# Recurrent mixer: three ScalarE roundings moved later, input-gate products and three low parts moved to GpSimd

## The chip, the cores and the metric

The kernel runs on one core of a Trainium2 chip as one program. The metric is the device time of one execution in microseconds, the median over several runs. The engines are TensorE (PE in the profile), VectorE (DVE), ScalarE (ACT), GpSimd (POOL) and the queue that issues most transfers (SyncE, SP).

## The reference, cut to what matters

A sequence of 256 positions with 1024 channels passes through a first block of two layers (an attention mixer, then a recurrent mixer, each followed by a feed-forward part) and a second block of two layers. All is float32. The change touches the recurrent mixer of the first block alone:

```
gate_branch, xr = jnp.split(x @ w_in, 2, axis=-1)
xr = causal_dwconv(xr, conv_w, conv_b)                 # 4 taps
r = sigmoid(blocks(xr) @ w_a + b_a)                    # recurrence gate
i = sigmoid(blocks(xr) @ w_x + b_x)                    # input gate
log_a = (-LRU_C * r) * softplus(-lam);  a = exp(log_a)
u = sqrt(-expm1(2.0 * log_a)) * (i * xr)
h = scan(h = a * h + u) over the positions
y = (h * gelu(gate_branch)) @ w_out
```

## The kernel before

Channels lie on the 128 partitions and the 256 positions on the free axis, so that a tensor of 1024 channels is eight tiles of 128x256. Each matrix product is done as three float32r products: weights and activations are split into a high part (rounded) and a low part (the remainder), and high x high, high x low and low x high are added in PSUM.

Weights come as 313 chunks of 128x2048, one MB each, through three raw buffers and a ring of four split buffers. SP issues the transfer of chunk n when the low part of chunk n-3 is written (it then owns the raw buffer). ScalarE rounds a chunk to its high part (`round_chunk`, line 224), VectorE subtracts (`rest_chunk`, line 233), and TensorE multiplies. `refill_hi(act, c)` rounds the chunk four after c, since it reuses the slot of c; `refill_lo(dve, c)` makes the low part of the chunk three after c. Every engine has one queue in program order, written out by hand, so a rounding that stands early in ScalarE's list holds all that stands behind it.

In the recurrent mixer TensorE does, in this order: four chunks `od_xr` (recurrent branch; chunks 53 to 56), `od_gate0` (57), two chunks `od_ax` (58, 59) with the gate matrices, in eight steps j of 12 matmuls each (6 for `r`, 6 for `i` of tile j), three chunks `od_gate` (60 to 62), and `od_out` (63 to 66). Step j > 3 reuses the PSUM bank of step j-4 and so waits for the sigmoid `i{j-4}`; it also waits for the low part of the branch, `lo{j//2}`. The first two chunks of `od_out` go through `alternating` (lines 291 and 298): all products with the high part of y, tile by tile, each waiting for `yhi`, then those with the low part, each waiting for `ylo`. They start when the low parts of both chunks 63 and 64 and `yhi0` are there. The next stage, `up1`, follows on TensorE without a pause.

`odd_act` is ScalarE's list (from line 1161): last taps, high parts of the branch (`xr_high`), sigmoids (line 1186), the group of Exp, Tanh and Square for each pair of tiles (lines 1231 to 1235), Sqrt (1238), Gelu (1191) and the high parts of y (1196), with the roundings between them. `odd_dve` is VectorE's (from line 1512): taps (1531), low parts of the branch (1537), `decay(j)` with the log of the decay `la` (1566) and the product of input gate and branch `ux` (1568), `v` (1578), `scan(h)` with `u` (1586) and two scans (1591), the gated output `y` (1597) and its low part (1602), with `take_scaled` (318, which empties a PSUM bank) and the low parts of the chunks between them. GpSimd does nothing in this stage. In the feed-forward stages it multiplies and makes low parts (lines 849, 855), and later it scales residuals (371).

Of the kernel before, what the change touches and what calls it, by code (L numbers as in the profile page):

```python
# [164 lines left out]
def program(nc, x_in, stream, par1_in, par2_in, ev_const, mask_const, mats, inv_in, out):  # L165
    with ExitStack() as ctx:
# [59 lines left out]
        def refill_hi(act, c):  # L226

            round_chunk(act, c.number + RING)
# [700 lines left out]
        def conv_names(g):  # L929
            return [f"{t}{d}_{g}" for d in (1, 2, 3) for t in "ab"]  # L930

        ax_names = [[f"r{j}", f"i{j}"] for j in range(8)]
        od_act = Steps(sem("od_act"), ["a_0", "b_0", "a_1", "b_1", "hi0", "hi1", "a_2", "b_2", "hi2", "a_3", "b_3"] +
                       sum(ax_names[:2], []) + ["hi3"] + sum(ax_names[2:], []) +
                       sum(([f"a{h}", f"tanh{h}", f"a2{h}"] for h in G4), []) + [f"sqrt{h}" for h in G4] +
                       ["gelu0", "gelu1", "yhi0", "yhi1", "gelu2", "yhi2", "gelu3", "yhi3"])
        od_dve = Steps(sem("od_dve"), conv_names(0) + conv_names(1) + ["lo0", "lo1"] + conv_names(2) + ["lo2"] +
                       conv_names(3) + ["lo3"] + sum(([f"la{j}", f"ux{j}"] for j in range(8)), []) +
                       [f"v{h}" for h in G4] +
                       ["u0", "scan00", "scan01", "u1", "scan10", "scan11", "y0", "y1", "ylo0",  # L940
                        "u2", "scan20", "scan21", "ylo1", "y2", "u3", "scan30", "scan31", "ylo2", "y3", "ylo3"])
        ax_done = sem("ax_step_done")

        def windows():
# [215 lines left out]
        def odd_act(act):  # L1160
# [53 lines left out]
            xr_high(2)  # L1214
            last_tap(3)
            act.activation(small[:, 6:7], eps, ACT.Sigmoid)
            act.wait_ge(chunk_done, gate0.number + 1)
            refill_hi(act, gate0)
            sigmoids(0)
            sigmoids(1)  # L1220
            xr_high(3)
            sigmoids(2)
            sigmoids(3)
            refill_hi(act, Chunk("od_ax", 0))
            for j in range(4, 8):
                sigmoids(j)
            refill_hi(act, Chunk("od_ax", 1))
            act.wait_ge(*A.after("i7"))
            for h in G4:
                act.wait_ge(*od_dve.after(f"ux{2 * h + 1}"))  # L1230
                act.activation(S(TMP + 2 * h, 2), S(RR + 2 * h, 2), ACT.Exp).then_inc(*A.did(f"a{h}"))
                act.activation(S(RR + 2 * h, 2), S(RR + 2 * h, 2), ACT.Tanh, scale=-1.0)\
                   .then_inc(*A.did(f"tanh{h}"))
                act.wait_ge(*A.after(f"a{h}"))
                act.activation(S(XC + 2 * h, 2), S(TMP + 2 * h, 2), ACT.Square).then_inc(*A.did(f"a2{h}"))
            for h in G4:
                act.wait_ge(*od_dve.after(f"v{h}"))
                act.activation(S(RR + 2 * h, 2), S(RR + 2 * h, 2), ACT.Sqrt).then_inc(*A.did(f"sqrt{h}"))
# [275 lines left out]
        def odd_dve(dve):  # L1514
            V = od_dve
            xr = [Chunk("od_xr", g) for g in G4]
            gate0 = Chunk("od_gate0", 0)
            gate = [Chunk("od_gate", g) for g in range(3)]

            def branch(g):  # L1520
                take_scaled(dve, xr[g], S(TMP + 2 * xr[g].slot, 2))

            def conv(g):
                dve.wait_ge(*od_act.after(f"b_{g}"))
                for d in (1, 2, 3):
                    for t, nm in enumerate("ab"):
                        k = 2 * g + t
                        if d > 1:
                            dve.wait_ge(*V.after(f"{nm}{d - 1}_{g}"))
                        w = PAR1["odw"] + 4 * k + 3 - d  # L1530
                        dve.scalar_tensor_tensor(out=scr[:, XC + k, d:T], in0=scr[:, TMP + 2 * xr[g].slot + t, 0:T - d],
                                                 scalar=par1[:, w:w + 1], in1=scr[:, XC + k, d:T],
                                                 op0=ALU.mult, op1=ALU.add).then_inc(*V.did(f"{nm}{d}_{g}"))

            def xr_low(g):
                dve.wait_ge(*od_act.after(f"hi{g}"))
                dve.tensor_tensor(hs[:, 8 + 2 * g:10 + 2 * g, 1, :], S(XC + 2 * g, 2),
                                  hs[:, 8 + 2 * g:10 + 2 * g, 0, :].bitcast(F32), ALU.subtract)\
                   .then_inc(*V.did(f"lo{g}"))

            refill_lo(dve, xr[0])
            inverse_dve(dve, N["mixnorm1"], 0)
            refill_lo(dve, xr[1])
            dve.wait_ge(*N["mixnorm1"]["stat"].after("copied"))
            branch(0)
            branch(1)
            conv(0)
            conv(1)
            xr_low(0)
            branch(2)  # L1550
            refill_lo(dve, xr[2])
            xr_low(1)
            conv(2)
            branch(3)
            refill_lo(dve, xr[3])
            xr_low(2)
            conv(3)
            take_scaled(dve, gate0, S(GB, 2))
            xr_low(3)
            refill_lo(dve, gate0)  # L1560
            cc = small[:, 24:32]

            def decay(j):

                dve.wait_ge(*od_act.after(f"i{j}"))
                dve.tensor_scalar(S1(RR + j), S1(RR + j), cc[:, j:j + 1], -8.0, ALU.mult, ALU.mult)\
                   .then_inc(*V.did(f"la{j}"))
                dve.tensor_tensor(S1(II + j), S1(II + j), S1(XC + j), ALU.mult).then_inc(*V.did(f"ux{j}"))
            for j in range(4):
                decay(j)  # L1570
            refill_lo(dve, Chunk("od_ax", 0))
            for j in range(4, 8):
                decay(j)
            refill_lo(dve, Chunk("od_ax", 1))
            for h in G4:

                dve.wait_ge(*od_act.after(f"a2{h}"))
                dve.scalar_tensor_tensor(out=S(RR + 2 * h, 2), in0=S(XC + 2 * h, 2), scalar=1.0,
                                         in1=S(RR + 2 * h, 2), op0=ALU.add, op1=ALU.mult).then_inc(*V.did(f"v{h}"))
                if h == 0:  # L1580
                    take_scaled(dve, gate[0], S(GB + 2, 2))
                    refill_lo(dve, gate[0])

            def scan(h):
                dve.wait_ge(*od_act.after(f"sqrt{h}"))
                dve.tensor_tensor(S(II + 2 * h, 2), S(II + 2 * h, 2), S(RR + 2 * h, 2), ALU.mult)\
                   .then_inc(*V.did(f"u{h}"))
                dve.wait_ge(*V.after(f"u{h}"))
                for k in range(2):
                    t = 2 * h + k  # L1590
                    dve.tensor_tensor_scan(S1(XC + t), S1(TMP + t), S1(II + t), 0.0, ALU.mult, ALU.add)\
                       .then_inc(*V.did(f"scan{h}{k}"))

            def gated(h):
                dve.wait_ge(*od_act.after(f"gelu{h}"))
                dve.wait_ge(*V.after(f"scan{h}1"))
                dve.tensor_tensor(S(GB + 2 * h, 2), S(GB + 2 * h, 2), S(XC + 2 * h, 2), ALU.mult)\
                   .then_inc(*V.did(f"y{h}"))

            def lo(h):  # L1600
                dve.wait_ge(*od_act.after(f"yhi{h}"))
                dve.tensor_tensor(hs[:, 2 * h:2 * h + 2, 1, :], S(GB + 2 * h, 2),
                                  hs[:, 2 * h:2 * h + 2, 0, :].bitcast(F32), ALU.subtract)\
                   .then_inc(*V.did(f"ylo{h}"))
            scan(0)
            take_scaled(dve, gate[1], S(GB + 4, 2))
            scan(1)
            refill_lo(dve, gate[1])
            gated(0)
            gated(1)  # L1610
            lo(0)
            scan(2)
            lo(1)
            gated(2)
            scan(3)
            take_scaled(dve, gate[2], S(GB + 6, 2))
            lo(2)
            gated(3)
            lo(3)
            refill_lo(dve, gate[2])  # L1620

        def pool_means(pool, l):

# [161 lines left out]
        def _(pool):  # L1785
# [14 lines left out]
            pool.wait_ge(*ev_dve.after("glo"))  # L1800
            pool.dma_start(S(INV, 4), inv_in).then_inc(inv_landed, 16)
            up_pool(pool, "up0", FF1, U["up0"], 0)
            up_pool(pool, "up1", FF1, U["up1"], 0)
            pool.wait_ge(inv_landed, 16)
            residual_pool(pool, PN["final"], 0, gains("final"))
# [9 lines left out]
        def _(pe):  # L1815
# [26 lines left out]
            for q in range(2):  # L1842
                c = Chunk("od_ax", q)
                pe.wait_ge(lo_ready, c.number + 1)
                for s in range(4):
# [6 lines left out]
                             signal=(chunk_done if s == 3 else ax_done, 1))  # L1852
            whole_pe(pe, "od_gate", 3, 0)
            out_pe(pe, "od_out", 1, hs, 8, lambda k: od_act.after(f"yhi{k // 2}"),
                   lambda k: od_dve.after(f"ylo{k // 2}"), 0, tr=O["od_out"])
            pre_pe(pe, [("up1", FF1)], N["ffnnorm1"], summed(O["od_out"]), 0)
            out_pe(pe, "down1", 3, hs, FF1, None, hs_ready(U["up1"], 0), 0, tr=O["down1"])

# [305 lines left out]
```

## Time and profile before

| what | value |
|---|---|
| median of 3 runs | 1913.71 us (1913.6 to 1913.81) |
| the profiled execution, own time | 1914.2 us |
| its span | 1912.4 us |
| mean granted TensorE clock | 0.987 of full |
| PE, DVE, ACT, POOL busy | 97%, 75%, 51%, 11% of the span |

The profiled execution took 1.8 us more than its span, and 0.5 us more than the median of the timed runs. Times in the rows below count from the start of the span. The recurrent mixer lies at about 396 to 476 us of it. Busy time of an engine is summed over its instructions. Successive instructions on one engine overlap a little, so the step from one start to the next is shorter than the duration shown.

### The profile page before, as it was taken

The numbers are of one execution on the slowest core, as the hardware profiler recorded it, in microseconds if no ns is written. First come the engines' busy times: TensorE is split into PE (matmuls) and PEld (weight loads), VectorE is DVE, ScalarE is ACT, GpSimd is POOL, SyncE is SP. The second block draws the span as 40 slices with busy tenths as digits, with TensorE's granted clock in tenths as the row PEclk, the third lists the DMA queues.
The fourth block names the chain that finished last, engine by engine and source line by source line (L and its number), as shares of the span: only waits on it lengthen the run. The fifth ranks groups of instructions, "written<-read, shape, count | busy, mean of one in ns | idle before, by whom it ended". The sixth has DMA issues, their size and how long they took to land.

```text
span 1912.4 us, 31584 instructions
## 1 busy us (share of the span) xinstructions
PE 1845.5 (97%) x13170; PEld 1730.8 (91%) x13170; DVE 1427.6 (75%) x1728; ACT 974.7 (51%) x1179; POOL 216.3 (11%) x160
## 2 busy tenths in 40 slices
PE   7978999999999999999999999999999999999997
PEld 7958999998999898889999988898889999998887
DVE  5796998578799568757875687758775886578774
ACT  5453765467666455544453455545554445345552
POOL 0020332000232012002300020002000220002000
PEclk9989999999999999999999999999999999999999
DMA  7413555534455545554454445554555445445551
GB/s 284 152 45 119 178 183 194 199 133 163 169 197 188 187 166 187 185 212 160 171 198 177 176 155 186 209 200 141 190 194 217 142 177 197 155 154 199 182 215 67
DMA packets 46788, 334.65 MB, mean 175 GB/s; under 512 B 5184, under 2 KB 5568, under 8 KB 6464
## 3 DMA queue, kind: packets, MB, share of 16 engines
q1 hardware_dynamic: 46512, 332.20, 48.2%
q8 instruction: 104, 1.70, 0.3%
q0 software_dynamic: 144, 0.52, 0.1%
q14 instruction: 28, 0.23, 0.0%
HBM read 331.65 MB, written 1.05 MB: 174 GB/s over the span
## 4 chain that ended last, share of the span: by engine, by line
PE 84%; DVE 11%; ACT 2%; issue 1%; DMA 1%; SPq 0%; DVEq 0%; ACTq 0%
PE psum L267 25%; PE psum L270 13%; PE psum L251 12%; PE psum L252 12%; PE psum L253 12%; PE psum L291 5%; DVE w_lo L233 3%; PE psum L298 3%; DMA w_raw<-stream_in 1%; DVE x_resid L476 1%; PE psum L585 1%; PE psum L584 1%; PE psum L582 1%; DVE x_split L408 1%; ACT w_hi L224 1%
## 5 line engine op out<-in xcount | busy, mean ns | idle before, releaser
L224 ACT ACTIVATE w_hi<-w_raw 128x2048 fp32r<-128x2048 f32 x313 | 598.2, 1912 | 459.5 <-PE psum L253 218.0
L233 DVE TENSOR_TENSOR w_lo<-w_raw,w_hi 128x2048 fp32r<-128x2048 f32 x313 | 726.6, 2324 | 44.1 <-ACT w_hi L224 44.1
L251 PE MATMUL psum<-x_split,w_hi 128*128 128x256 f32 x1768 | 504.4, 285 | 11.8 <-DVE x_split L408 10.5
L252 PE MATMUL psum<-x_split,w_hi 128*128 128x256 f32 x1768 | 500.9, 283 | 0.0
L253 PE MATMUL psum<-x_split,w_lo 128*128 128x256 f32 x1768 | 500.8, 283 | 0.0
L267 PE MATMUL psum<-x_split,w_hi 128*128 128x512 f32 x1216 | 430.2, 399 | 3.5 <-DVE scratch L318 3.5
L251 PEld LDWEIGHTS psum<-x_split,w_hi 128*128 128x128 f32 x1768 | 339.9, 192 | 13.9 <-issue 12.8
L270 PE MATMUL psum<-x_split,w_lo 128*128 128x256 f32 x1216 | 341.5, 281 | 0.0
L252 PEld LDWEIGHTS psum<-x_split,w_hi 128*128 128x128 f32 x1768 | 339.9, 192 | 0.1
L253 PEld LDWEIGHTS psum<-x_split,w_lo 128*128 128x128 f32 x1768 | 339.9, 192 | 0.0
L267 PE MATMUL psum<-h_split,w_hi 128*128 128x512 f32 x816 | 288.6, 399 | 0.0
L267 PEld LDWEIGHTS psum<-x_split,w_hi 128*128 128x128 f32 x1216 | 228.5, 188 | 61.1 <-DVE scratch L318 4.3
L270 PEld LDWEIGHTS psum<-x_split,w_lo 128*128 128x128 f32 x1216 | 229.7, 189 | 0.0
L270 PE MATMUL psum<-h_split,w_lo 128*128 128x256 f32 x816 | 229.2, 281 | 0.0
L267 PEld LDWEIGHTS psum<-h_split,w_hi 128*128 128x128 f32 x816 | 153.3, 188 | 38.2
L371 POOL TENSOR_TENSOR x_resid<-x_resid,squares 128x512 f32<-128x512 f32 x24 | 63.0, 2655 | 873.1 <-DVE squares L360 873.0
L270 PEld LDWEIGHTS psum<-h_split,w_lo 128*128 128x128 f32 x816 | 154.1, 189 | 0.0
L318 DVE TENSOR_TENSOR scratch<-psum,inv_rms 128x512 f32<-128x512 f32 (+1 forms) x129 | 86.8, 682 | 76.0 <-PE psum L253 75.8
L251 PE MATMUL psum<-h_split,w_hi 128*128 128x256 f32 x480 | 138.7, 289 | 3.9 <-issue 2.0
L748 ACT ACTIVATE scratch<-psum 128x512 f32<-128x512 f32 x76 | 45.4, 598 | 187.1 <-PE psum L270 187.1
L252 PE MATMUL psum<-h_split,w_hi 128*128 128x256 f32 x480 | 136.9, 285 | 0.0
L253 PE MATMUL psum<-h_split,w_lo 128*128 128x256 f32 x480 | 136.8, 285 | 0.0
(233 smaller groups left out, 2434.6 us busy)
## 6 DMA issues: line engine op xcount, KB each, us to landing
w_raw<-stream_in SPq DMA_DIRECT2D x313, 1024.0 KB, 4.8
x_resid<-x_in SPq DMA_DIRECT2D x1, 1024.0 KB, 7.0
y_out<-x_resid SPq DMA_DIRECT2D x4, 256.0 KB, 2.5
scratch<-mask_in SPq DMA_DIRECT2D x1, 768.0 KB, 11.0
scratch<-ev_in SPq DMA_DIRECT2D x1, 512.0 KB, 9.6
scratch<-inv_in POOLq DMA_DIRECT2D x1, 512.0 KB, 3.9
params<-par_in SPq DMA_DIRECT2D x1, 247.0 KB, 7.1
matrices<-mat_in SPq DMA_DIRECT2D x1, 192.0 KB, 8.9
```

Of the source, the lines that this page charges most:

```text
L224: act.activation(w_hi[:, n % RING, :], raw[:, n % RAWS, :], ACT.Copy).then_inc(hi_ready, 1)
L233: dve.tensor_tensor(w_lo[:, n % RING, :], raw[:, n % RAWS, :], w_hi[:, n % RING, :].bitcast(F32), ALU.subtract).then_inc(lo_ready, 1)
L251: pe.matmul(dst, w_hi[:, c.slot, b:b + P], src[:, k0 + k, 0, :], start=opens, stop=False)
L252: pe.matmul(dst, w_hi[:, c.slot, b:b + P], src[:, k0 + k, 1, :], start=False, stop=False)
L253: done = pe.matmul(dst, w_lo[:, c.slot, b:b + P], src[:, k0 + k, 0, :], start=False, stop=last and k == nk - 1 and m == len(tiles_) - 1)
L267: pe.matmul(ps[:, bank_, :], w_hi[:, c.slot, b:b + P], src[:, k0 + k, :, :].rearrange("p a t -> p (a t)"), start=first and k == 0, stop=False)
L270: done = pe.matmul(tile(bank_, 0), w_lo[:, c.slot, b:b + P], src[:, k0 + k, 0, :], start=False, stop=last and k == nk - 1)
L291: pe.matmul(tile(c.bank, m), w[:, c.slot, b:b + P], src[:, k0 + k, 0, :], start=k == 0 and m == 0 and w is w_hi, stop=False)
L298: done = pe.matmul(tile(c.bank, m), w_hi[:, c.slot, b:b + P], src[:, k0 + k, 1, :], start=False, stop=k == nk - 1 and m == 1)
L318: dve.tensor_tensor(dst, bank(c.bank, tiles), rinv[:, :].unsqueeze(1).to_broadcast([P, tiles, T]), ALU.mult).then_inc(pair_taken, 1)
L371: pool.tensor_tensor(x[:, 2 * g:2 * g + 2, :], x[:, 2 * g:2 * g + 2, :], UNRMS.unsqueeze(1).to_broadcast([P, 2, T]), ALU.mult).then_inc(*t ...
L748: act.activation(S(ACC + 2 * c.slot, 2), ps[:, c.bank:c.bank + 2, T:2 * T], ACT.Copy)\
```

## The change

On ScalarE the roundings of chunks 61, 62 and 63 (`refill_hi` of `gate0`, `od_ax` 0 and 1) stand later: 61 behind all four of the first sigmoid pairs and `xr_high(3)`, 62 behind the Exp group of pair 1, and 63 behind that of pair 2. The Exp groups wait for `la` in place of `ux`, and the Square, which overwrites the branch, waits for `ux`.

The product `ux` leaves VectorE for GpSimd, one instruction of 128x256 for each of eight tiles, each waiting for its sigmoid `i{j}`. `la` now waits for `r{j}` alone. VectorE's low parts of chunks 60 to 63 move within its list: 60 behind the first four `la`, 61 behind the other four, 62 behind `v1` and the emptying of the first gate bank, 63 behind `v2`. Each scan also waits for GpSimd's product.

Of the four low parts of y, GpSimd makes the first three (128x512 each), VectorE the last. `gated(0)` stands ahead of the low part of chunk 64 instead of behind it, and the emptying of the last gate bank ahead of scan 3.

```diff
@@ odd_act
             act.activation(small[:, 6:7], eps, ACT.Sigmoid)
+            for j in range(4):
+                sigmoids(j)
+            xr_high(3)
             act.wait_ge(chunk_done, gate0.number + 1)
             refill_hi(act, gate0)
-            sigmoids(0)
-            sigmoids(1)
-            xr_high(3)
-            sigmoids(2)
-            sigmoids(3)
-            refill_hi(act, Chunk("od_ax", 0))
             for j in range(4, 8):
                 sigmoids(j)
-            refill_hi(act, Chunk("od_ax", 1))
-            act.wait_ge(*A.after("i7"))
             for h in G4:
-                act.wait_ge(*od_dve.after(f"ux{2 * h + 1}"))
+                act.wait_ge(*od_dve.after(f"la{2 * h + 1}"))
                 ...
                 act.wait_ge(*A.after(f"a{h}"))
+                act.wait_ge(*od_pool.after(f"ux{2 * h + 1}"))
                 act.activation(S(XC + 2 * h, 2), S(TMP + 2 * h, 2), ACT.Square).then_inc(*A.did(f"a2{h}"))
+                if h == 1:
+                    refill_hi(act, Chunk("od_ax", 0))
+                if h == 2:
+                    refill_hi(act, Chunk("od_ax", 1))
@@ odd_dve
             xr_low(3)
-            refill_lo(dve, gate0)
 ...
-                dve.wait_ge(*od_act.after(f"i{j}"))
+                dve.wait_ge(*od_act.after(f"r{j}"))
                 dve.tensor_scalar(S1(RR + j), ..., ALU.mult, ALU.mult).then_inc(*V.did(f"la{j}"))
-                dve.tensor_tensor(S1(II + j), S1(II + j), S1(XC + j), ALU.mult).then_inc(*V.did(f"ux{j}"))
             for j in range(4):
                 decay(j)
-            refill_lo(dve, Chunk("od_ax", 0))
+            refill_lo(dve, gate0)
             for j in range(4, 8):
                 decay(j)
-            refill_lo(dve, Chunk("od_ax", 1))
+            refill_lo(dve, Chunk("od_ax", 0))
             for h in G4:
                 ...                                    # v{h}
-                if h == 0:
+                if h == 1:
                     take_scaled(dve, gate[0], S(GB + 2, 2))
+                    refill_lo(dve, Chunk("od_ax", 1))
+                if h == 2:
                     refill_lo(dve, gate[0])
             def scan(h):
                 dve.wait_ge(*od_act.after(f"sqrt{h}"))
+                dve.wait_ge(*od_pool.after(f"ux{2 * h + 1}"))
 ...
             scan(1)
+            gated(0)
             refill_lo(dve, gate[1])
-            gated(0)
             gated(1)
-            lo(0)
             scan(2)
-            lo(1)
             gated(2)
+            take_scaled(dve, gate[2], S(GB + 6, 2))
             scan(3)
-            take_scaled(dve, gate[2], S(GB + 6, 2))
-            lo(2)
             gated(3)
-            lo(3)
+            ...                                        # ylo3, as lo(3) was
+        def odd_pool(pool):
+            for j in range(8):
+                pool.wait_ge(*od_act.after(f"i{j}"))
+                pool.tensor_tensor(S1(II + j), S1(II + j), S1(XC + j), ALU.mult).then_inc(*od_pool.did(f"ux{j}"))
+            for h in range(3):
+                pool.wait_ge(*od_act.after(f"yhi{h}"))
+                pool.tensor_tensor(hs[:, 2 * h:2 * h + 2, 1, :], S(GB + 2 * h, 2),
+                                   hs[:, 2 * h:2 * h + 2, 0, :].bitcast(F32), ALU.subtract)\
+                    .then_inc(*od_pool.did(f"ylo{h}"))
@@ gpsimd
             up_pool(pool, "up0", FF1, U["up0"], 0)
+            odd_pool(pool)
             up_pool(pool, "up1", FF1, U["up1"], 0)
```

## Rows read from the trace of the kernel before

**Rows 1.** The page, parts 1 and 4: busy time, chain of waits by engine.
```profile
PE 1845.5 (97%) x13170; PEld 1730.8 (91%) x13170; DVE 1427.6 (75%) x1728; ACT 974.7 (51%) x1179; POOL 216.3 (11%) x160
...
PE 84%; DVE 11%; ACT 2%; issue 1%; DMA 1%; SPq 0%; DVEq 0%; ACTq 0%
```

**Rows 2.** Timeline, TensorE: start us, us, instruction, [idle before <-releaser].
```profile
421.85 0.36 PE L251 MATMUL psum<-h_split,w_hi 128*128 128x256 f32 x1 [2.02 <-issue]
...
429.14 0.28 PE L251 MATMUL psum<-x_split,w_hi 128*128 128x256 f32 x1
...
450.55 0.46 PE L291 MATMUL psum<-h_split,w_hi 128*128 128x256 f32 x1 [3.97 <-ACT h_split L1196]
...
458.83 0.38 PE L291 MATMUL psum<-h_split,w_hi 128*128 128x256 f32 x1 [0.81 <-ACT h_split L1196]
```

**Rows 3.** Windows of 1 us: busy of PE, PEld, DVE, ACT, POOL, clock, DMA share, GB/s.
```profile
425.00:426.00 1.00, 1.00 (x7) 1.00 (x6) 1.00 (x2) 1.00 (x1) 0.00 (x0) 0.50 0.06 16
...
451.00:452.00 1.00, 1.00 (x7) 1.00 (x6) 0.96 (x3) 1.00 (x1) 0.00 (x0) 0.50 0.77 319
```

**Rows 4.** Timeline, ScalarE, same columns.
```profile
419.13 1.89 ACT L224 ACTIVATE w_hi<-w_raw 128x2048 fp32r<-128x2048 f32 x1
420.93 1.55 ACT L1186 ACTIVATE scratch<-psum,params 128x256 f32<-128x256 f32 x4
422.36 0.64 ACT L1176 ACTIVATE h_split<-scratch 128x512 fp32r<-128x512 f32 x1
...
432.84 1.28 ACT L1231 ACT_TABLE_LOAD   x1
...
441.81 2.19 ACT L1238 ACTIVATE scratch<-scratch 128x512 f32<-128x512 f32 x4
...
458.15 0.63 ACT L1196 ACTIVATE h_split<-scratch 128x512 fp32r<-128x512 f32 x1 [0.76 <-DVE scratch L1597]
```

**Rows 5.** Timeline, VectorE, same columns.
```profile
419.30 2.44 DVE L1531 SCALAR_TENSOR_TENSOR scratch<-scratch,params 128x255 f32<-128x255 f32 x6
...
423.64 2.29 DVE L233 TENSOR_TENSOR w_lo<-w_raw,w_hi 128x2048 fp32r<-128x2048 f32 x1
425.84 0.35 DVE L1566 TENSOR_SCALAR scratch<-scratch,small 128x256 f32<-128x256 f32 x1
426.11 0.42 DVE L1568 TENSOR_TENSOR scratch<-scratch 128x256 f32<-128x256 f32 x1
426.44 0.34 DVE L1566 TENSOR_SCALAR scratch<-scratch,small 128x256 f32<-128x256 f32 x1
...
439.25 1.97 DVE L1578 SCALAR_TENSOR_TENSOR scratch<-scratch 128x512 f32<-128x512 f32 x3
442.47 0.69 DVE L1586 TENSOR_TENSOR scratch<-scratch 128x512 f32<-128x512 f32 x1 [1.25 <-ACT scratch L1238]
...
450.44 0.69 DVE L1602 TENSOR_TENSOR h_split<-scratch,h_split 128x512 fp32r<-128x512 f32 x1
451.05 0.69 DVE L1586 TENSOR_TENSOR scratch<-scratch 128x512 f32<-128x512 f32 x1
```

**Rows 6.** Timeline, GpSimd, same columns.
```profile
502.08 2.61 POOL L849 TENSOR_TENSOR scratch<-scratch 128x256 f32<-128x256 f32 x1 [175.61 <-ACT scratch L726]
...
620.94 0.74 POOL L855 TENSOR_TENSOR h_split<-scratch,h_split 128x256 fp32r<-128x256 f32 x1 [0.53 <-ACT h_split L732]
621.64 2.79 POOL L849 TENSOR_TENSOR scratch<-scratch 128x256 f32<-128x256 f32 x1
...
898.46 1.30 POOL L371 TENSOR_TENSOR x_resid<-x_resid,squares 128x512 f32<-128x512 f32 x1
```

**Rows 7.** Timeline, VectorE, beside instructions of GpSimd.
```profile
501.64 2.45 DVE L799 SCALAR_TENSOR_TENSOR scratch<-scratch,params 128x254 f32<-128x254 f32 x6
504.01 0.69 DVE L318 TENSOR_TENSOR scratch<-psum,inv_rms 128x512 f32<-128x512 f32 x1
...
621.01 2.82 DVE L233 TENSOR_TENSOR w_lo<-w_raw,w_hi 128x2048 fp32r<-128x2048 f32 x1
...
723.86 3.38 DVE L233 TENSOR_TENSOR w_lo<-w_raw,w_hi 128x2048 fp32r<-128x2048 f32 x1
```

**Rows 8.** The page, part 6: transfers, KB each, us to landing.
```profile
w_raw<-stream_in SPq DMA_DIRECT2D x313, 1024.0 KB, 4.8
```

More of the change, by code:

```diff
@@ L933, in program @@
         od_act = Steps(sem("od_act"), ["a_0", "b_0", "a_1", "b_1", "hi0", "hi1", "a_2", "b_2", "hi2", "a_3", "b_3"] +
-                       sum(ax_names[:2], []) + ["hi3"] + sum(ax_names[2:], []) +
+                       sum(ax_names[:4], []) + ["hi3"] + sum(ax_names[4:], []) +
                        sum(([f"a{h}", f"tanh{h}", f"a2{h}"] for h in G4), []) + [f"sqrt{h}" for h in G4] +
@@ L937, in program @@
         od_dve = Steps(sem("od_dve"), conv_names(0) + conv_names(1) + ["lo0", "lo1"] + conv_names(2) + ["lo2"] +
-                       conv_names(3) + ["lo3"] + sum(([f"la{j}", f"ux{j}"] for j in range(8)), []) +
+                       conv_names(3) + ["lo3"] + [f"la{j}" for j in range(8)] +
                        [f"v{h}" for h in G4] +
-                       ["u0", "scan00", "scan01", "u1", "scan10", "scan11", "y0", "y1", "ylo0",
-                        "u2", "scan20", "scan21", "ylo1", "y2", "u3", "scan30", "scan31", "ylo2", "y3", "ylo3"])
+                       ["u0", "scan00", "scan01", "u1", "scan10", "scan11", "y0", "y1",
+                        "u2", "scan20", "scan21", "y2", "u3", "scan30", "scan31", "y3", "ylo3"])
+        od_pool = Steps(sem("od_pool"), [f"ux{j}" for j in range(8)] + ["ylo0", "ylo1", "ylo2"])
         ax_done = sem("ax_step_done")
@@ L1598, in gated @@
                    .then_inc(*V.did(f"y{h}"))
[L1600 to L1604, printed above, removed]
             scan(0)
@@ L1607, in odd_dve @@
             scan(1)
+            gated(0)
             refill_lo(dve, gate[1])
-            gated(0)
             gated(1)
-            lo(0)
             scan(2)
-            lo(1)
             gated(2)
+            take_scaled(dve, gate[2], S(GB + 6, 2))
             scan(3)
-            take_scaled(dve, gate[2], S(GB + 6, 2))
-            lo(2)
             gated(3)
-            lo(3)
+            dve.wait_ge(*od_act.after("yhi3"))
+            dve.tensor_tensor(hs[:, 6:8, 1, :], S(GB + 6, 2), hs[:, 6:8, 0, :].bitcast(F32), ALU.subtract)\
+               .then_inc(*V.did("ylo3"))
             refill_lo(dve, gate[2])
+        def odd_pool(pool):
[7 more added lines that the diff above has]
+                    .then_inc(*od_pool.did(f"ylo{h}"))
         def pool_means(pool, l):
@@ L1854, in _ @@
             out_pe(pe, "od_out", 1, hs, 8, lambda k: od_act.after(f"yhi{k // 2}"),
-                   lambda k: od_dve.after(f"ylo{k // 2}"), 0, tr=O["od_out"])
+                   lambda k: od_dve.after("ylo3") if k // 2 == 3 else od_pool.after(f"ylo{k // 2}"), 0,
+                   tr=O["od_out"])
             pre_pe(pe, [("up1", FF1)], N["ffnnorm1"], summed(O["od_out"]), 0)
```

## The prediction

> **What bounds the kernel now.** I read the busy shares first, then the chain of waits, then the stage itself engine by engine. TensorE is busy 97% of the span and 84% of the chain that ended last is its own [rows 1], so another engine matters only where TensorE stands idle, and this kernel can gain from the change only what TensorE idles in the recurrent mixer.
>
> TensorE's timeline shows three such places [rows 2]: 2.02 us before the second half of the gate matrices (421.85), 3.97 us before the output projection (450.55) and 0.81 us inside it (458.83). From 458.83 on it runs without a pause into the next stage. So what sets the time of the whole kernel is the start at 458.83: 16 matmuls that wait for the last high part of y, which ScalarE makes at 458.15 and ends at 458.78 [rows 4]. The two earlier pauses are worth nothing by themselves. If this start moves by d, the end moves by d, as all behind it (weights, transfers, next stage) follows TensorE. The quantity to forecast is d.
>
> Behind 458.15 stands VectorE. It is busy almost without a break from 442.47 to the last gated output, and at 442.47 it had idled 1.25 us for ScalarE's Sqrt [rows 5], which began at 441.81 [rows 4]. So d = (shift of the first u at 442.47) + (change in VectorE's own list from there on).
>
> **Front part, ScalarE.** The first sigmoid stands behind a rounding (419.13, next start 420.93 [rows 4]), 1.80 us from start to start. Without it the sigmoids begin at 419.13. Four of them take 422.36 - 420.93 = 1.43, 0.36 each, so eight end their issue at 422.0; the taps end at 419.30 + 2.44 = 421.74 [rows 5], so the high part of the branch starts at 422.0 in place of 422.36. TensorE's second half of the gate matrices waited for the sigmoid i0 (it is the first that 421.85 can wait for) and starts near 420.1; 24 matmuls at 0.12 (the 144 of the three gate chunks run from 429.14 to 450.55 - 3.97 = 446.58 [rows 2], 17.4 / 144) to 423.0, then the low part of the branch at 423.35, then 24 more to 426.4. The last sigmoids end at 427.3. The table load for Exp starts then, against 432.84 [rows 4], 5.5 us earlier. Two roundings now stand inside the Exp groups, 2 x 1.80 = 3.6. Sqrt would start at 441.81 - 5.5 + 3.6 = 439.9, 1.9 us earlier.
>
> **Front part, VectorE.** It loses eight products: from product to next instruction 426.44 - 426.11 = 0.33 [rows 5], 2.6 us together, all in this part. The price is on GpSimd, and no row shows these products there, but the nearest rows do. Alone, 256 elements take 0.74 and 512 take 1.30 [rows 6]. Not alone, the two engines exclude each other whenever VectorE reads two operands from SBUF. The product at 621.64 took 2.79: VectorE's low part ran from 621.01 to 623.83, and GpSimd ended 0.60 after it. That same low part took 2.82 in place of 2.29, 0.53 more, as GpSimd's instruction of 620.94 was under way [rows 5 to 7]. With 512 elements the toll is 3.38 - 2.29 = 1.1 [rows 5, 7]. Beside VectorE instructions that read PSUM neither pays (1.30 at 898.46, 0.69 at 504.01). So each product of 256 costs VectorE 0.55 where it is busy and 0 where it idles: the bounds for eight are 0 and 4.4 us, against 2.6 removed.
>
> The Trainium skill (SBUF — State Buffer, section Who interferes with whom) says that a VectorE instruction with two SBUF inputs contends with a GpSimd instruction that reads SBUF, as an exclusive lock in which the other side fully blocks. The trace agrees, with 0.53 and 1.1 us above. It speaks against this change: work handed to GpSimd is still paid by VectorE, at a longer hold. By a page that knew no lock the forecast would be the first rival below.
>
> I take nearly the upper bound, as VectorE is busy throughout here. Walk: after the low part of the branch VectorE is free at 423.3. Four `la` at 0.27 are 1.1, five products fall among them and before the low part of chunk 60 (5 x 0.55 = 2.75), that low part 2.2: ready at 429.3, where it was ready at 425.9. TensorE wants it at 426.4, so its first gate chunk now runs 429.4 to 435.3 (before: from 429.14 [rows 2], so this costs nothing). Then VectorE empties that bank (0.6), makes low part 62 (2.2), `v2` (0.64, from 1.97 for three less the overlap), low part 63 (2.2), `v3` (0.64): 441.7. The first u starts at 441.7, against 442.47: -0.75 us. ScalarE's Sqrt at 439.9 is no longer the bound. Without any toll it would be, u at 440.6, -1.8 us; with the toll falling also on the taps, -0.6 to 0. The transfer of chunk 63 is issued after low part 60, 429.3 + 4.8 [rows 8] = 434.1, and ScalarE wants it at 435.1: covered by 1.0 us. Chunk 64 has over 3 us, the others more.
>
> How GpSimd's first product after a long pause behaves is open: at 502.08 it took 2.61, with six VectorE taps of two SBUF inputs beside it, which were not slowed (2.45 for six), and ended 0.67 after 504.01, where VectorE went to PSUM [rows 6, 7]. Either it starts slowly or it was kept out. Both give the same here: the first product ends at about 422.8, behind the taps, and these are not hit. If it is quick, see the second rival.
>
> **Back part.** VectorE loses three low parts of y, 451.05 - 450.44 = 0.61 each [rows 5], 1.8 us, and a wait of about 0.2 before the last gated output. GpSimd makes them at 512 elements, a toll of 1.1 each while VectorE is busy, and it is: 3.3 us. The bounds are 0 and 3.3; I take 3.3, as all three fall beside gated outputs and scans (two SBUF operands). Scans beside GpSimd appear in no row, and I treat them like the others. Net +1.3. Moving `gated(0)` ahead of low part 64 changes the order but not the sum: yhi0 is ready near 447.5 instead of 450.41, and TensorE then waits for low part 64, 449.1. Its start moves 1.3 us forward, and it ends these 48 matmuls near 457.4, waiting as before.
>
> **Sum.** d = -0.75 + 1.3 = +0.55 us, say +0.6. Against the profiled execution, 1914.2 + 0.6 = 1914.8; the timed runs lie 0.5 below it, so the median is forecast at 1913.71 + 0.6 = 1914.3 us. What the measurement tells from no change, 0.2%, is 3.8 us: this is "same", with its own range -0.8 to +1.6 (1912.9 to 1915.3). Chance 0.50.
>
> **Rivals.**
> 1. *The toll is small* (GpSimd's instructions fall into VectorE's idle time, or scans and `la` don't exclude it). Then u starts 1.8 us earlier; the first gated output waits about 0.7 for Gelu; the back part gives 2.0 (1.8 + 0.2). Sum -3.1 at the last high part, of which TensorE takes -2.8 since its 48 matmuls end only then: 1910.9. For it: VectorE waits on ScalarE in the front part once it has fewer instructions. Against: both rows with VectorE's low part. Chance 0.22.
> 2. *GpSimd's first products hit the taps.* Slower. Place: 420.0 to 421.7, four to six taps. Price: two to three tolls of 0.55, high part and low part of the branch 1.0 to 1.5 us late, and all behind them, sum +1.6; TensorE's pause before the last 16 matmuls grows to some 2.1 us. It decides if the first product ends before 421.7. Against: the 2.61 us of 502.08. A pause of 2.02 us at 421.85 was followed by half clock (0.50 at 425 us [rows 3], 1.2 GHz), a step of some 0.21 instead of 0.12. If that happens on this stretch, where TensorE itself is the bound, it costs about 16 x 0.09 = 1.5 more, if 16 matmuls go at half clock: +3.1, 1916.8. Chance 0.12.
> 3. *The clock alone.* As forecast, but the pause before the last 16 matmuls (459.4 - 457.4 = 2.0 us, before 0.81) lets the clock fall behind it: +0.6 + 1.5 = +2.1, 1915.8. For it: the 2.02 us pause. Against: two pauses with half clock behind them (425 and 451 us [rows 3]) are few cases, the shorter as long as this one. Chance 0.16.
>
> The Trainium skill (TensorE: Matmul & The Clock Gate, section What's actually happening) says that the clock falls back after idling and that the moment is not tied to the program. The two cases here agree that it falls after a pause, and can't show the second. No term above needs it.
>
> **How the numbers follow.** The range holds 8 in 10: from a bit inside rival 1 to a bit inside rival 2: 1910.8 to 1916.5. Faster by over 0.2% needs d below -3.8: rival 1 and something more, 0.07. Slower by over 0.2% needs d above +3.8: rival 2 with the clock and more, 0.07. Same 0.86.
>
> **What would show it.** In the profile after: VectorE's `la` and low part 60 longer by 0.55 or multiples, low part 60 ending near 429.3; first u at 441.7; GpSimd's low parts of y at 1.3 to 2.6 us, and beside each a gated output or scan 1.1 us longer; TensorE's last start at 459.4 in place of 458.83; its first start at 449.2. Undisturbed VectorE durations, or a first u at 440.6, would prove the forecast wrong towards rival 1. Taps above 0.5 us would show rival 2, a clock of 0.50 behind the last start rival 3.

## The result, and the profile after

The changed kernel takes 1918.65 us (median of 9 runs, 1914.83 to 1920.37), the kernel before 1913.92 us beside it (9 runs, 1913.6 to 1916.46): ratio 1.0019, 95% interval 1.0011 to 1.0028. By the medians it is slower by 4.7 us, by the ratio by 3.6 (2.1 to 5.4), where +0.6 was forecast; the median lies above the range (1910.8 to 1916.5). Its runs fall into two groups, 1914.8 to 1915.5 (three) and 1918.0 to 1920.4 (six). The profiled execution took 1920.37, span 1918.6, which is 6.2 more than the span of before (1912.4), so it belongs to the second group.

The page of the changed kernel, parts 1 and 4, against [rows 1]: VectorE has 11 instructions fewer and is busy 2.7 us more, though those 11 cost it some 4.5 us before (8 x 0.33 and 3 x 0.61 [rows 5]).

```profile
PE 1847.3 (96%) x13170; PEld 1732.6 (90%) x13170; DVE 1430.3 (75%) x1717; ACT 974.6 (51%) x1179; POOL 229.7 (12%) x171
...
PE 84%; DVE 11%; ACT 3%; DMA 1%; issue 1%; SPq 0%; DVEq 0%; ACTq 0%
```

Timeline, TensorE, changed kernel (start us, us, instruction, [idle before <-releaser], here and in all timelines), against [rows 2]. The first, third and fourth line are the starts of 421.85, 450.55 and 458.83 there. The second, the branch's last 24 matmuls, had no pause before it in the kernel before.

```profile
419.92 0.36 PE L251 MATMUL psum<-h_split,w_hi 128*128 128x256 f32 x1 [0.22 <-issue]
...
425.08 0.36 PE L251 MATMUL psum<-h_split,w_hi 128*128 128x256 f32 x1 [2.04 <-DVE h_split L1538]
...
452.18 0.55 PE L291 MATMUL psum<-h_split,w_hi 128*128 128x256 f32 x1 [5.22 <-DVE w_lo L233]
...
462.34 0.39 PE L291 MATMUL psum<-h_split,w_hi 128*128 128x256 f32 x1 [2.07 <-ACT h_split L1197]
```

Timelines of VectorE and of GpSimd, changed kernel, against [rows 5]:

```profile
419.17 4.37 DVE L1532 SCALAR_TENSOR_TENSOR scratch<-scratch,params 128x255 f32<-128x255 f32 x6
...
428.10 2.58 DVE L1566 TENSOR_SCALAR scratch<-scratch,small 128x256 f32<-128x256 f32 x4
430.59 2.84 DVE L233 TENSOR_TENSOR w_lo<-w_raw,w_hi 128x2048 fp32r<-128x2048 f32 x1
...
443.73 0.69 DVE L1588 TENSOR_TENSOR scratch<-scratch 128x512 f32<-128x512 f32 x1 [0.61 <-ACT scratch L1239]
...
449.03 0.69 DVE L1599 TENSOR_TENSOR scratch<-scratch 128x512 f32<-128x512 f32 x1 [0.82 <-ACT scratch L1192]
...
451.84 1.76 DVE L1599 TENSOR_TENSOR scratch<-scratch 128x512 f32<-128x512 f32 x1
...
454.24 2.31 DVE L1593 TENSOR_TENSOR_SCAN scratch<-scratch 128x256 f32<-128x256 f32 x2
...
458.58 2.25 DVE L1593 TENSOR_TENSOR_SCAN scratch<-scratch 128x256 f32<-128x256 f32 x2
```

```profile
419.90 3.36 POOL L1622 TENSOR_TENSOR scratch<-scratch 128x256 f32<-128x256 f32 x4 [93.57 <-ACT scratch L1187]
426.81 3.45 POOL L1622 TENSOR_TENSOR scratch<-scratch 128x256 f32<-128x256 f32 x3 [3.55 <-ACT scratch L1187]
...
450.47 2.59 POOL L1625 TENSOR_TENSOR h_split<-scratch,h_split 128x512 fp32r<-128x512 f32 x1 [19.18 <-ACT h_split L1197]
454.35 1.65 POOL L1625 TENSOR_TENSOR h_split<-scratch,h_split 128x512 fp32r<-128x512 f32 x1 [1.29 <-ACT h_split L1197]
458.09 1.61 POOL L1625 TENSOR_TENSOR h_split<-scratch,h_split 128x512 fp32r<-128x512 f32 x1 [2.09 <-ACT h_split L1197]
```

These lines show what GpSimd costs VectorE. The six taps took 4.37 in place of 2.44 with four products inside them. Three products made four `la` 2.58 long (1.14 without, at 424.85 in this trace), and one made the low part 2.84 (2.29 before). Three low parts of y lie beside the gated output of 451.84 (1.76 for 0.69) and two pairs of scans (2.31 and 2.25 for 1.27).

Earlier stages shift from one execution to the next, so I count in every trace from the first of these taps to TensorE's last start in the mixer, and call it the mixer's time. Before: 458.83 - 419.30 = 39.53 us. Changed: 462.34 - 419.17 = 43.17, 3.6 more. Behind that start the 1 us windows of the changed kernel (busy PE, PEld, DVE, ACT, POOL; clock; DMA share; GB/s) show half clock. The first line shows that the pause of 2.04 us was followed by it too:

```profile
427.00:428.00 1.00, 1.00 (x7) 1.00 (x6) 1.00 (x1) 1.00 (x4) 1.00 (x1) 0.50 0.00 0
...
464.00:465.00 1.00, 1.00 (x7) 1.00 (x7) 1.00 (x1) 0.10 (x1) 0.00 (x0) 0.50 0.00 0
465.00:466.00 1.00, 1.00 (x6) 1.00 (x6) 0.21 (x1) 0.00 (x0) 0.00 (x0) 0.50 0.00 0
...
467.00:468.00 1.00, 1.00 (x9) 1.00 (x9) 0.00 (x0) 0.00 (x0) 0.00 (x0) 0.89 0.78 303
```

Next stage's first matmul starts at 481.21, before 476.20: +5.0. So 3.5 came up to the last start and 1.5 with the clock behind it. The last 1.2 are the net of stretches that the change doesn't touch. The next block opens with a pause of 2.25 us in both executions (up to 877.06 before, 882.08 changed); behind it TensorE went at half clock in the kernel before and at full clock in the changed one. The changed one then paused 1.62 us at 895.43 for a low part and went at half clock at 898 us, where the kernel before had neither. By 1054 us it was 6.5 behind, at the end 6.2.

```profile
898.00:900.00 2.00, 2.00 (x12) 2.00 (x11) 2.00 (x3) 0.88 (x1) 2.00 (x1) 0.50 0.76 320
```

### The profile page after: what moved, and what is told of

Same layout as the page of the kernel before. It is cut to its first block, busy times and chain, and to the rows that moved or that the text cites. A ratio compares the mean times of both kernels' runs of the same rounds, so it can differ in the third digit from the quotient of the medians.

```text
span 1918.6 us, 31591 instructions
## 1 busy us (share of the span) xinstructions
PE 1847.3 (96%) x13170; PEld 1732.6 (90%) x13170; DVE 1430.3 (75%) x1717; ACT 974.6 (51%) x1179; POOL 229.7 (12%) x171
## 3 DMA queue, kind: packets, MB, share of 16 engines
HBM read 331.65 MB, written 1.05 MB: 173 GB/s over the span
## 4 chain that ended last, share of the span: by engine, by line
PE 84%; DVE 11%; ACT 3%; DMA 1%; issue 1%; SPq 0%; DVEq 0%; ACTq 0%
PE psum L267 25%; PE psum L270 13%; PE psum L251 12%; PE psum L253 12%; PE psum L252 12%; PE psum L291 5%; DVE w_lo L233 3%; PE psum L298 2%; DVE x_resid L476 1%; ACT w_hi L224 1%; DMA w_raw<-stream_in 1%; DVE x_split L408 1%; PE psum L585 1%; PE psum L584 1%; PE psum L582 1%
```

## The experiments

Each median stands with its ratio to the kernel before on the same chip and the 95% interval of that ratio; "+x" behind a mixer's time is against 39.53. The first matmul of the next stage, counted from the same tap, takes the clock behind the last start in as well: 56.90 us before (476.20 - 419.30), 62.04 in the changed kernel (481.21 - 419.17).

**1. The new order alone.** The products and the low parts go back to VectorE, ScalarE's list and the other moves stay, GpSimd idles.

```diff
+ dve.tensor_tensor(S1(II + j), S1(II + j), S1(XC + j), ALU.mult)   # behind each la{j}
+ lo(0) .. lo(2) on dve, each in its place of before
- odd_pool(pool)
```

> The changed kernel with the eight products of input gate and branch and the three low parts of y back on VectorE; the new places of ScalarE's roundings, of VectorE's low parts and of the gated output are kept. GpSimd does nothing in this stage. Theory 1 (GpSimd's two-operand instructions hold up VectorE's two-operand instructions, 0.5 us for 256 elements and 1.1 us for 512, and that made the 3.5 us by which the last high part of y was late): taps back to 2.4 us for six, last start of the output projection near 457.4 us against 458.8 before and 462.3 in the changed kernel, so 1 to 2 us faster than the kernel before. Rival A (the new order of roundings and low parts is what costs): still 3 to 5 us slower than before. Rival B (the whole loss is TensorE's clock falling in a pause): taps and scans as in the changed kernel's lists don't matter, time between 0 and +1.5 us by the clock behind the last start alone.

1912.44 us, 0.9993 [0.9984, 1.0002]. Mixer 419.60 to 458.01 = 38.41 (-1.1). The reordering is no loss. Timeline, VectorE: the taps are whole, scans undisturbed.

```profile
419.60 2.45 DVE L1532 SCALAR_TENSOR_TENSOR scratch<-scratch,params 128x255 f32<-128x255 f32 x6
...
441.10 0.69 DVE L1589 TENSOR_TENSOR scratch<-scratch 128x512 f32<-128x512 f32 x1 [0.33 <-ACT scratch L1239]
...
451.14 1.27 DVE L1594 TENSOR_TENSOR_SCAN scratch<-scratch 128x256 f32<-128x256 f32 x2
```

**2. Only the low parts on GpSimd**, the products back on VectorE.

```diff
- for j in range(8): pool.tensor_tensor(... ux{j})
+ dve.tensor_tensor(... ux{j}) behind each la{j}
```

> The changed kernel with only the eight products back on VectorE; GpSimd still makes three low parts of y. Theory 1: taps undisturbed (2.4 us for six), the first u near 441.2, but one gated output and two pairs of scans each 1.05 us longer, last start near 458.9, so 0 us against the kernel before, up to +1.5 where the clock falls behind the last start. Rival A: 3 to 5 us slower. Rival B: 0 to +1.5.

1914.65 us, 1.0009 [1.0, 1.0018]: 2.2 above experiment 1. Mixer 418.44 to 458.54 = 40.10 (+0.6). The second gated output took 1.77, the scans 2.31 and 2.25, as in the changed kernel.

**3. Only the products on GpSimd**, the low parts back on VectorE.

```diff
- for h in range(3): pool.tensor_tensor(... ylo{h})
+ lo(0) .. lo(2) on dve, each in its place of before
```

> The changed kernel with only the three low parts of y back on VectorE; GpSimd still makes the eight products. Theory 1: the six taps take 4.4 us, as in the changed kernel, and the first u is near 443, later than before by 1.2; gated outputs and scans are undisturbed, and the tail is 3.3 - 1.8 = 1.5 shorter than in the changed kernel, so the last start is near 459 to 460, 0 to +1 us against before, up to 1.5 more with the clock. Rival A: 3 to 5 us slower. Rival B: 0 to +1.5.

1913.66 us, 1.0001 [0.9992, 1.001]: 1.2 above experiment 1. Mixer 418.92 to 458.57 = 39.65 (+0.1). One expectation missed: in this execution the taps were not hit. Timelines of VectorE and GpSimd: the first four products took 4.90 and ended behind the taps.

```profile
418.92 2.46 DVE L1532 SCALAR_TENSOR_TENSOR scratch<-scratch,params 128x255 f32<-128x255 f32 x6
...
419.67 4.90 POOL L1629 TENSOR_TENSOR scratch<-scratch 128x256 f32<-128x256 f32 x4 [93.56 <-ACT scratch L1187]
```

The halves add 2.2 and 1.2 to experiment 1, and the whole change adds about 6 (+4.7 and -1.4, each against the kernel before in its own set). By the ratios the halves add 3.1 and 1.5 to experiment 1, and the whole change about 5.0, so it is not shown that together they cost more than the two apart.

**4. The products wait for the taps.**

```diff
  def odd_pool(pool):
+     pool.wait_ge(*od_dve.after("b3_3"))
      for j in range(8):
```

> The changed kernel with one more wait: GpSimd's first product waits for VectorE's last tap. Theory 1: six taps take 2.4 us, high part of the branch back to 422.0; the products then fall beside the log decays and low part 60, where VectorE has about 1 us to spare, so the last start moves from 462.3 to about 460.5: 1 to 2 us faster than the changed kernel, 1 to 2 slower than before. If the collision with the taps is not what made the front late (rival A), the time is that of the changed kernel.

1915.23 us (1914.31 to 1917.21), 1.001 [1.0001, 1.0019]: by the medians 3.3 of the 4.7 us are gone, by the ratios 1.7 of 3.6, with intervals that overlap. None of its 11 runs reaches 1918 us, which six of nine of the changed kernel do. Mixer 418.40 to 459.91 = 41.51 (+2.0), 1.7 less than in the changed kernel. VectorE, and TensorE with its window:

```profile
422.83 2.58 DVE L1566 TENSOR_SCALAR scratch<-scratch,small 128x256 f32<-128x256 f32 x4
425.33 2.83 DVE L233 TENSOR_TENSOR w_lo<-w_raw,w_hi 128x2048 fp32r<-128x2048 f32 x1
...
435.83 0.69 DVE L318 TENSOR_TENSOR scratch<-psum,inv_rms 128x512 f32<-128x512 f32 x1 [2.26 <-PE psum L253]
```

```profile
428.30 0.43 PE L251 MATMUL psum<-x_split,w_hi 128*128 128x256 f32 x1 [2.13 <-DVE w_lo L233]
...
429.00:430.00 1.00, 1.00 (x6) 1.00 (x6) 1.00 (x3) 1.00 (x3) 0.49 (x1) 0.50 0.96 139
...
464.00:465.00 1.00, 1.00 (x11) 1.00 (x10) 0.00 (x0) 0.00 (x0) 0.00 (x0) 1.00 0.60 180
```

TensorE waited 2.13 us for low part 60 and then went at half clock, so VectorE waited 2.26 us for the bank of the first gate chunk. The three chunks took 19.0 us (428.30 to 447.31), 17.4 before. Behind the last start (459.91, pause 2.10) the clock stayed full here.

**5. Idle work on GpSimd, nothing else changed.** To the kernel before: eight products of 256 elements and three of 512, of constants, released by the same steps of ScalarE; nobody uses their results.

```diff
+ for j in range(8): pool.wait_ge(*od_act.after(f"i{j}"));   pool.tensor_tensor(... 256 elements)
+ for h in range(3): pool.wait_ge(*od_act.after(f"yhi{h}")); pool.tensor_tensor(... 512 elements)
```

> The kernel before, every list as it was, with eleven instructions added on GpSimd whose results nobody uses: eight of 128x256 (product of two constants in SBUF) released by the sigmoids i0 to i7, three of 128x512 released by the first three high parts of y. No other engine waits for them. Theory 1 (two-operand instructions of the two engines exclude each other): VectorE's instructions from 422 us on are stretched by 0.5 us for each of the eight, of which about 1.2 is hidden by its wait for Sqrt, and by 1.05 for each of the three: 3 + 3 = 5 to 6.5 us slower than before. Rival A (the order of the lists is the cause) and rival B (clock alone): within 0.5 us of before, as no list and no wait is changed.

1919.82 us (1919.65 to 1921.82, 5 runs), 1.0034 [1.0021, 1.0048]. Mixer 419.13 to 463.00 = 43.87 (+4.3); the next stage's first matmul comes 62.74 behind the first tap (+5.8). The taps are whole (2.45), as the first idle product starts only at 421.73. VectorE's list is that of before, and its instructions are stretched (0.83 against 0.34 [rows 5], 1.78 against 0.69, 2.35 against 1.27):

```profile
425.84 0.83 DVE L1567 TENSOR_SCALAR scratch<-scratch,small 128x256 f32<-128x256 f32 x1
...
451.99 1.78 DVE L1587 TENSOR_TENSOR scratch<-scratch 128x512 f32<-128x512 f32 x1
...
453.81 2.35 DVE L1592 TENSOR_TENSOR_SCAN scratch<-scratch 128x256 f32<-128x256 f32 x2
```

So the toll is shown without any change of order or of a wait: work that nobody needs, on an engine 11% busy, costs 6 us. A small toll, the first rival, is refuted.

**6. Experiment 4 with 16 matmuls of filler** into the chunk's own bank, which the chunk then opens anew, ahead of TensorE's wait for low part 60, so that it doesn't idle there.

```diff
+ if ph == "od_gate" and c.n == 0:
+     for _ in range(16): pe.matmul(tile(c.bank, 0), xs[:, 0, 0, 0:P], xs[:, 0, 0, :], start=True, stop=True)
```

> The kernel in which GpSimd's products wait for the taps, with 16 matmuls more on TensorE ahead of its wait for low part 60 (into the bank that the gate chunk then opens anew). In that kernel TensorE paused 2.13 us there and then ran the first gate chunk in 7.5 us in place of 5.8, and VectorE waited 2.26 us for it. Theory 1c (half clock behind this pause is why the front part came out 1.2 us later than my walk): the pause is nearly filled, the chunk takes 5.8 us, the first u comes 1 to 1.5 us earlier counted from the first tap of group 3, and the time falls by about 1.2 us to 0.2 us above the kernel before. Rival (the walk missed something else in VectorE's list): no change.

1914.94 us, 1.0006 [0.9997, 1.0015]. The clock stayed full, the gate chunks took 17.5 us (428.69 to 446.23), VectorE waited 0.70 for the bank instead of 2.26, and the mixer took 418.88 to 459.43 = 40.55 (+1.0): half clock behind that pause is worth 1.0 us of the mixer. The medians of 4 and 6 differ by 0.3 only, less than the 1.2 expected and less than two medians can tell.

```profile
434.75 0.69 DVE L318 TENSOR_TENSOR scratch<-psum,inv_rms 128x512 f32<-128x512 f32 x1 [0.70 <-PE psum L253]
```

**7. The same filler also before the last high part.**

```diff
+ if first.phase == "od_out" and k == 6:
+     for _ in range(16): pe.matmul(ps[:, 7, 0:T], ...)
```

> The same, with 16 matmuls more ahead of TensorE's wait for the last high part of y (into an unused bank). Theory 1c: the stretch behind the last start runs at full clock in every run; it removes the part of the spread that comes from there. Median the same as with one filler or up to 1 us lower, spread smaller. If TensorE comes late at that point (pause under 1.9 us), the filler costs what it exceeds the pause by, at most 1 us.

1914.99 us (1912.16 to 1916.97), 1.0007 [0.9998, 1.0016]. The pause shrank to 0.18, the mixer stayed at 40.53, and the median didn't move. The profiled execution of 6 had full clock behind this start already, so its filler had nothing to remove there. The spread did not shrink as expected (4.8 us between the extremes, 3.5 in experiment 6). Inconclusive on the price of that pause.

**8. Experiment 1 with the low parts of y last on VectorE**, behind the last gated output, since TensorE takes them only behind the high parts.

```diff
- lo(0), lo(1), lo(2) between the scans
+ for h in G4: lo(h)      # behind gated(3)
```

> The new lists with all work on VectorE (as in the first experiment), and the low parts of y for the first three pairs moved behind the last gated output, since TensorE wants them only 1.9 us after its last start. VectorE's list ahead of the last gated output is 1.8 us shorter. Theory 1: last high part 1.8 us earlier than in the first experiment; TensorE then ends its first 48 matmuls about when it comes, so the last start gains 1.1 to 1.8 us and no pause is left there: 2.5 to 3 us faster than the kernel before. If low parts were not on the path that sets the end, no change against the first experiment (1.4 faster than before).

1911.61 us, 0.9987 [0.9978, 0.9996]. That is 2.1 us by the medians where 2.5 to 3 were expected. TensorE's 64 matmuls now run without a pause, 448.68 to 457.93, and the next stage starts 54.37 us behind the first tap, in experiment 1 55.79: 1.4 us come from the low parts' place.

```profile
454.34 0.69 DVE L1600 TENSOR_TENSOR scratch<-scratch 128x512 f32<-128x512 f32 x1
454.95 2.49 DVE L1605 TENSOR_TENSOR h_split<-scratch,h_split 128x512 fp32r<-128x512 f32 x4
```

**9. The same, with low part 64 again ahead of the first gated output.**

```diff
+ refill_lo(dve, gate[1])
  gated(0)
- refill_lo(dve, gate[1])
```

> The last experiment's kernel (new lists, all work on VectorE, low parts of y last) with the low part of chunk 64 back ahead of the first gated output, as in the kernel before, so that it fills VectorE's wait of 0.8 us for Gelu. Theory 1 with TensorE's start as the new bound: TensorE's first start of the output projection 0.4 us earlier, the last gated output 0.8 us earlier; the 64 matmuls run without a pause, so the end gains 0.4 us, up to 1 more or less by when the clock comes back: 2.2 to 3 us faster than before. Rival (VectorE still sets the end): 0.8 us.

1911.06 us (1907.63 to 1911.71), 0.9984 [0.9975, 0.9993]: 2.9 us under the kernel before and the lowest median of this study. It has nothing on GpSimd in this stage. In the profile the next stage starts 54.36 behind the first tap, as in experiment 8 (54.37), so the gain over 8 isn't shown: TensorE began 0.4 earlier and then took 9.45 us in place of 9.09 for the 64 matmuls, with some 3 us at half clock in both.

**10. The same, with 20 matmuls of filler before the output projection.**

```diff
+ if c.phase == "od_out" and c is first: 20 x pe.matmul(tile(c.bank, 0), ...)
```

> The same, with 20 matmuls more ahead of TensorE's wait for the first start of the output projection (into the bank that it then opens anew). Theory 1c: TensorE's pause of 3 us there is filled with 2.4 us of work, the clock stays up, and the 64 matmuls take 7.7 in place of 9.2 us: 1 to 1.5 us faster than without the filler, 3.5 to 4.5 faster than before. If the clock falls all the same, no change against the kernel without filler.

1911.24 us, 0.9985 [0.9976, 0.9994]. Missed. TensorE kept full clock at 452 us, where experiment 9 shows 0.50, and then caught up with VectorE and waited 1.12 for the last high part:

```profile
456.60 0.39 PE L294 MATMUL psum<-h_split,w_hi 128*128 128x256 f32 x1 [1.12 <-ACT h_split L1200]
```

**11 and 12. The changed kernel profiled twice more**, as nothing else tells whether the taps are hit each time.

> The changed kernel as it is, profiled again. Its timed runs lie in two groups, 1914.8 to 1915.5 and 1918.0 to 1920.4 us. Theory 1b: the groups differ by whether GpSimd's first products get in between VectorE's taps. Below 1916 us the six taps take 2.45 us and GpSimd's first product waits some 1.5 us for them; above 1918 us they take about 4.4 us. Rival: the taps take 4.4 us in both and the groups come from the clock alone.

> The same once more, for a profile of the other group. Theory 1b and the rival as for the run before.

Run 11, 1917.49 us, mixer 419.58 to 460.90 = 41.32 (+1.8), taps spared:

```profile
419.58 2.45 DVE L1532 SCALAR_TENSOR_TENSOR scratch<-scratch,params 128x255 f32<-128x255 f32 x6
...
420.32 4.91 POOL L1622 TENSOR_TENSOR scratch<-scratch 128x256 f32<-128x256 f32 x4 [93.57 <-ACT scratch L1187]
...
436.84 0.69 DVE L318 TENSOR_TENSOR scratch<-psum,inv_rms 128x512 f32<-128x512 f32 x1 [2.24 <-PE psum L253]
```

Run 12, 1919.33 us, mixer 419.08 to 462.34 = 43.26 (+3.7), taps hit:

```profile
419.08 4.38 DVE L1532 SCALAR_TENSOR_TENSOR scratch<-scratch,params 128x255 f32<-128x255 f32 x6
...
419.81 3.37 POOL L1622 TENSOR_TENSOR scratch<-scratch 128x256 f32<-128x256 f32 x4 [93.57 <-ACT scratch L1187]
```

The same program has both courses, though GpSimd starts 0.73 to 0.74 us behind the first tap in all three executions. So the taps are worth 1.9 us of the mixer (41.3 spared, 43.2 hit, one and two executions), and experiment 4, which spares them by a wait, agrees with 1.7. They don't alone make the two groups of timed runs: with spared taps I expected under 1916 and got 1917.49, between the groups, with half clock behind the last start again.

## Why the prediction was wrong, step by step

**The bound and the method were right.** The next stage followed TensorE's last start in the mixer (+3.5), and what came on top of it there is the clock (+1.5).

**The toll was right, in kind and size.** Forecast 0.55 and 1.1 us, for the eight products at most 4.4. Measured for the eight: 1.93 + 1.44 + 0.55 = 3.9. Four products add 4.37 - 2.44 = 1.93 to the taps (0.48 each), three add 2.58 - 1.14 = 1.44 to the `la`, one adds 2.84 - 2.29 = 0.55 to the low part, and those of 512 elements add 1.07, 1.04 and 0.98. Scans pay like the others, which no row had shown.

**The step that failed first: "the first product ends at about 422.8, behind the taps, and these are not hit".** It was read from one row, the 2.61 us at 502.08 [rows 6]. In two of three profiles of the changed kernel four products went in among the taps, and the branch's high part came 1.2 us late (423.57 for 422.36). Then TensorE paused 2.04 us before the branch's last 24 matmuls, fell to half clock and took 425.08 to 429.39 = 4.3 for them instead of 2.9. ScalarE waited for them with the last two sigmoids, and its list moved: Exp's table load at 430.49 (forecast 427.3), Sqrt at 443.06 (forecast 439.9). Of these 3.2, 1.7 are a later start (425.08, forecast 423.35) and 1.4 the clock. The first u came at 443.73, where VectorE waited for ScalarE's Sqrt, which the prediction had taken off the path: 24.56 us behind the first tap, before 23.17. The timeline of ScalarE, changed kernel:

```profile
423.57 0.63 ACT L1177 ACTIVATE h_split<-scratch 128x512 fp32r<-128x512 f32 x1 [1.56 <-DVE scratch L1532]
...
429.63 0.84 ACT L1187 ACTIVATE scratch<-psum,params 128x256 f32<-128x256 f32 x2 [1.43 <-PE psum L253]
430.49 1.28 ACT L1227 ACT_TABLE_LOAD   x1
...
443.06 2.19 ACT L1239 ACTIVATE scratch<-scratch 128x512 f32<-128x512 f32 x4
```

That is the second rival, with the chance 0.12; experiment 4 and runs 11 and 12 put 1.7 to 1.9 us on it.

**The second failed step: the first gate chunk "now runs 429.4 to 435.3", "so this costs nothing".** The time of low part 60 was right: ready 9.76 us behind the first tap in experiment 4 (418.40 to 428.16), 10.0 forecast. But the chunk was priced at full clock, though the same text has TensorE idle from 426.4 to 429.4 and expects half clock behind pauses as long elsewhere. Experiment 4 against 6: u comes 23.64 us behind the first tap with half clock and 22.09 with full; before 23.17. So the forecast of -0.75 for u held at full clock only (-1.1), and half clock made +0.5 of it. This step bites where the taps are spared (run 11: a pause of 2.19 before 429.33); where they are hit, the delay comes earlier and TensorE goes from the gate matrices into the chunk without a pause (429.39).

**The back part, +1.3 forecast.** From u to the last start it took 16.36 us before [rows 2, 5], 17.87 in experiment 4 (+1.5) and 18.61 in the changed kernel (+2.25). The tolls were 3.1 there (1.07 + 1.04 + 0.98) and the three low parts gone 1.8, as forecast; what I left out is that the first gated output waits for Gelu (0.82 at 449.03), which I counted in rival 1 only. Experiment 4, with no such wait, comes out near the forecast.

**The clock behind the last start** (rival 3, 0.16) cost 1.5 in the profiled execution, as priced there. Runs 11 and 12 and experiment 2 (pauses of 2.10 and 2.11 us) have it too, and experiment 5 (2.76); experiments 4 and 6, with a pause of 2.10 each, don't. The Trainium skill (TensorE: Matmul & The Clock Gate, section What's actually happening) says that the moment of the fall isn't tied to the program. The trace agrees: pauses of 2.07 us (changed) and 2.10 us (experiment 4) at the same instruction, clock 0.50 behind the one and 1.00 behind the other.

**The transfers** stayed covered, as said: no wait of these stretches ends on one.

**Summed**, for the profiled execution: front part +1.4 (forecast -0.75), back part +2.2 (forecast +1.3), clock behind the last start +1.5 (forecast 0), another half-clock stretch outside the mixer +1.2. These are 6.3, against 6.2 between the spans (and 0.1 that the first tap came earlier). I held the mishaps to be separate and gave each a small chance. Two of them are one chain: the toll on the taps makes a TensorE pause, the pause brings half clock, and the clock passes the delay on. The pause of 2.1 us before the last start is another matter: it comes with the low parts on GpSimd, with the taps hit or not (2.11 in experiment 2, 2.10 in 4 and in run 11; 1.10 in experiment 1 and 1.52 in 3, which have the low parts on VectorE). Open are two things: what decides whether GpSimd gets in among the taps, and how much of the difference between the two groups of timed runs is taps and how much clock.

## What to carry to other kernels

Work moved to GpSimd beside a busy VectorE is still paid by VectorE when both read SBUF, at 0.5 us for 256 elements and 1.05 for 512, which here is more than the 0.33 and 0.61 it costs on VectorE itself. Price a move by what GpSimd's requests will fall beside, and price a new TensorE pause like those here (2.0 to 2.2 us) with half clock behind it, 1.0 to 1.5 us. Before work is moved to another engine, look whether it can go later on its own: the same low parts, last on VectorE, gave 1.4 us between the profiles of experiments 1 and 8, and with the new order of the lists 2.9 us against the kernel before in experiment 9.

## What the runs showed of the hardware that was not expected

- Between VectorE instructions that follow each other without a gap, GpSimd gets in or is kept out, in the same program: taps 4.37 and 4.38 with products of 0.84 each, or 2.45 with the first products ending only behind the taps (the changed kernel and run 12 against run 11 and experiment 3). The same holds beside a low part of a chunk: at 430.5 the product took 0.74 and the low part 2.84 in the first profile of the changed kernel, 2.85 and 2.28 in run 12.
- VectorE's scale by one scalar column (TENSOR_SCALAR), with one full input, pays too: 0.83 for 0.34 (experiment 5). So do scans: 2.31 for 1.27.
- The length of a pause doesn't settle the clock behind it. Pauses of 2.04 to 2.13 us were followed by half clock in most cases (425, 428 and 462 us), not in experiments 4 and 6 before the last start. Before the output projection 3.02 us was followed by it in experiment 7 and not in 6, and 2.42 us in run 11 and not in experiment 3. One of 1.62 us was (895.43, changed kernel), one of 1.49 us in experiment 1 (428.44) was not. Such half-clock stretches cover 3 to 4 windows of 1 us. With the 5.22 us before the output projection of the changed kernel, it began within the pause and went on to 457 us.
